# First MLP product of an encoder layer by one level of Strassen's scheme, with its result kept in DRAM between the two MLP products

## The reference

```python
h2 = rms_norm(x, norm_mlp_g)
x = x + jnp.square(jax.nn.relu(h2 @ w_mlp1)) @ w_mlp2
```

## Time and profile before

| | |
|---|---|
| runs | 2709.89, 2710.58, 2710.71 us; median 2710.58 us |
| profiled execution | 2709.54 us, of it a span of 2708.0 us that the records cover |
| PE busy | 2679.5 us (99%), weight loads 2322.8 us (86%) |
| DVE busy | 1210.4 us (45%) |
| ACT busy | 967.7 us (36%) |
| POOL busy | 150.9 us (6%) |
| granted TensorE clock | 0.999 |

### The profile page before, as it was taken

How to read it: one execution, slowest core, us unless ns; L and a number is a source line. 1 busy time by engine, 2 the same in 40 slices (tenths; PEclk the granted TensorE clock), 3 DMA queues, 4 the chain that set the end, 5 groups by cost and what they waited for, 6 DMA issues and landing times.

```text
span 2708.0 us, 39414 instructions
## 1 busy us (share of the span) xinstructions
PE 2679.5 (99%) x14690; PEld 2322.8 (86%) x14690; DVE 1210.4 (45%) x2015; ACT 967.7 (36%) x1645; POOL 150.9 (6%) x246
## 2 busy tenths in 40 slices
PE   7999999999999999999999999999999999999998
PEld 6888888889888888888888888888888888888887
DVE  4335433364333643345353534544445444544733
ACT  5554245443454434543352425211221122111531
POOL 3001000100001000100100010000000000000000
PEclk9999999999999999999999999999999999999999
DMA  3122122221222221221433222111111111111122
GB/s 112 25 32 71 42 71 32 31 73 43 62 32 33 71 74 31 33 54 59 183 120 119 87 86 62 40 39 39 38 33 39 38 39 39 39 39 39 33 67 64
DMA packets 174756, 153.10 MB, mean 57 GB/s; under 512 B 12352, under 2 KB 153216, under 8 KB 174624
## 3 DMA queue, kind: packets, MB, share of 16 engines
q1 hardware_dynamic: 156672, 95.05, 12.8%
q0 software_dynamic: 15872, 56.20, 7.4%
q10 hardware_dynamic: 2080, 0.14, 0.1%
HBM read 127.44 MB, written 23.74 MB: 56 GB/s over the span
## 4 chain that ended last, share of the span: by engine, by line
PE 97%; DVE 1%; ACT 1%; issue 1%; DMA 0%; SPq 0%; POOL 0%; ACTq 0%; DVEq 0%; POOLq 0%
PE bank L771 28%; PE bank L773 28%; PE bank L772 28%; PE bank L886 2%; PE bank L867 1%; PE bank L969 1%; PE bank L956 1%; PE bank L877 1%; PE bank L929 1%; PE bank L965 1%; PE bank L854 1%; PE bank L841 1%; PE bank L839 1%; DVE act_lo L1907 0%; PE bank L794 0%
## 5 line engine op out<-in xcount | busy, mean ns | idle before, releaser
L771 PE MATMUL bank<-act_hi,w_hi 128*128 128x512 f32 (+1 forms) x3192 | 1175.1, 368 | 0.7 <-DVE act_lo L1586 0.7
L773 PE MATMUL bank<-act_hi,w_lo 128*128 128x512 f32 (+1 forms) x3192 | 1131.9, 355 | 0.0
L772 PE MATMUL bank<-act_lo,w_hi 128*128 128x512 f32 (+1 forms) x3192 | 1131.2, 354 | 0.0
L773 PEld LDWEIGHTS bank<-act_hi,w_lo 128*128 128x128 f32 x3192 | 602.4, 189 | 86.4
L771 PEld LDWEIGHTS bank<-act_hi,w_hi 128*128 128x128 f32 x3192 | 603.7, 189 | 77.9 <-DVE act_lo L1586 0.9
L772 PEld LDWEIGHTS bank<-act_lo,w_hi 128*128 128x128 f32 x3192 | 604.6, 189 | 73.7
L1144 ACT ACTIVATE w_hi<-w_raw 128x1024 fp32r<-128x1024 f32 (+1 forms) x173 | 178.9, 1034 | 407.4 <-PE bank L773 387.1
L1561 DVE TENSOR_TENSOR w_lo<-w_raw,w_hi 128x1024 fp32r<-128x1024 f32 (+1 forms) x175 | 209.9, 1200 | 179.3 <-ACT w_hi L1144 178.4
L1960 DVE TENSOR_TENSOR work<-bank,work 128x512 f32<-128x512 f32 (+1 forms) x384 | 226.6, 601 | 129.4 <-PE bank L773 126.4
L771 PE MATMUL bank<-u_hi,w_hi 128*128 128x512 f32 (+1 forms) x768 | 272.3, 355 | 0.0
L772 PE MATMUL bank<-u_lo,w_hi 128*128 128x512 f32 (+1 forms) x768 | 272.0, 354 | 0.0
(11 more groups left out here) (262 smaller groups left out, 2476.6 us busy)
## 6 DMA issues: line engine op xcount, KB each, us to landing
w_raw<-in_w_in_dram SPq DMA_DIRECT2D x76, 512.0 KB
w_raw<-in_w_mlp_dram SPq DMA_DIRECT2D x64, 512.0 KB
work<-gate_scratch POOLq DMA_DIRECT2D x16, 640.0 KB, 5.6
gate_scratch<-work POOLq DMA_DIRECT2D x15, 640.0 KB, 3.3
work<-weight_scratch POOLq DMA_DIRECT2D x12, 640.0 KB, 5.9
oa_scratch<-work POOLq DMA_DIRECT2D x8, 640.0 KB, 4.7
work<-oa_scratch POOLq DMA_DIRECT2D x8, 640.0 KB, 12.6
x_in<-in_x_sample_dram SPq DMA_DIRECT2D x8, 512.0 KB, 7.7
```

Of the source, the lines that this page charges most:

```text
L771: nc.tensor.matmul(out, wh, rh, start=first and k == 0, stop=False, skip_group_check=True)
L772: nc.tensor.matmul(out, wh, rl, start=False, stop=False, skip_group_check=True)
L773: mm = nc.tensor.matmul(out, wl, rh, start=False, stop=k == kt - 1, skip_group_check=True)
```

## The change

With the 1024 inputs, the hidden features and the tokens each cut in two halves, a product of 2 x 2 blocks takes seven products of sums of blocks instead of eight. Here one pair i of hidden tiles (2 x 128 features), all 1280 tokens and all 1024 inputs is such a 2 x 2 product. There are 16 pairs and so 112 products g; each has 4 input tiles, 128 features and 640 tokens as 2 x 320 columns: 4 x 2 x 3 = 24 matmuls of 320 columns.

The seven products (numbered m as Strassen's) need sums and differences of the halves of h (x times `g_mlp`) and of the weights:

- Activations, once: `x_rows` lists the two halves; DVE (`piece_sum`) makes them for m = 4, 3 and 1, POOL for m = 7 and 6 (eight additions of 128 x 640), m = 2 and 5 are halves of h as they are. ACT makes the high parts (`piece_high`) and DVE the low parts (`piece_low`). They lie where `act_hi` and `act_lo` were; for m = 4 and 2 in rows 8 to 15 of `work`, and most of these are made during the eight tiles of `merged @ w_out`.
- Weights, for each product: two raw slabs of a pair lie in `w_raw` and `raw_1` (which is slot 0 of `w_hi`). `weight_sum` (DVE, 128 x 512), `weight_high` (ACT) and `weight_low` (DVE) fill one of three slots of `ring`, two products ahead. SP loads the next pair's slabs, `w_raw` first, once the last weight sum of the pair is made.
- Results: four quarters of a pair lie in `kept`, four rows of 640 in `work` rows 16 and 17. A product is in two PSUM banks; with 8 banks four products can be in flight. ACT copies the first use (`kept_copy`), DVE adds or subtracts the others (`added`). A finished quarter gets max and `r_bc` from DVE (`finals`), is squared by ACT, and POOL stores it to `u_scratch` in DRAM.
- x + merged @ w_out is stored to `x1_scratch` during the eight tiles and h is written over it; x is loaded back to `xres` in 14 half rows, seven at g = 56 and seven at g = 108. In `mlp_round` DVE waits for all of them.
- The second product follows in 16 rounds of two slabs. Each round's 256 rows of u (1280 KB) are loaded from DRAM by POOL, split by ACT (`u_highs`) and DVE (`u_lows`). Round 0's are loaded at g = 106; round 1's and 2's behind the last product and the last stores.
- The sum of squares is now in `r_bc`, and its matmuls (`squares_summed`) use banks 6, 7 and 6; PE waits for ACT's Ln before each reuse.

The core of the diff:

```diff
+            for i in range(PAIRS):
+                for m in (1, 0):
+                    if i:
+                        sp.wait_ge(sw_sum, sums_of(7 * i - 1) + 1)
...
+                    sp.dma_start((w_raw if m else raw_1)[:].rearrange("p (k n) -> p k n", n=P),
+                                 w_1[:, :, (2 * i + m) * P:(2 * i + m + 1) * P]).then_inc(raw_loaded[m], 16)
...
+                def part(a, j):
+                    hi, lo = x_operand(m, a)
+                    out = bank[2 * (g % 4) + j][:, 0:320]
+                    wh, wl = w[:, 0, a * P:a * P + P], w[:, 1, a * P:a * P + P]
+                    nc.tensor.matmul(out, wh, hi[:, j, :], start=a == 0, stop=False, skip_group_check=True)
+                    nc.tensor.matmul(out, wh, lo[:, j, :], start=False, stop=False, skip_group_check=True)
+                    return nc.tensor.matmul(out, wl, hi[:, j, :], start=False, stop=a == 3, skip_group_check=True)
...
+            s_product(0)
+            pe.wait_ge(x1_acc, KT + 4)
+            squares_summed(0, 6)
+            squares_summed(1, 7)
+            s_product(1)
+            pe.wait_ge(w2_read, 2)
+            squares_summed(2, 6)
+            s_product(2)
+            pe.wait_ge(w2_read, 4)
+            for g in range(3, PRODUCTS):
+                s_product(g)
...
+            for g in range(PRODUCTS + 1):
+                if g:
+                    kept_copy(g - 1)
+                if g == 1:
+                    root_part(0, 6)
+                    root_part(1, 7)
...
+                if g + 2 < PRODUCTS:
+                    weight_high(g + 2)
+                if g < 4:
...
+                    for pair in range(4):
+                        piece_high((1, 7, 6, 5)[g], pair)
...
+            for g in range(PRODUCTS + 1):
+                if g + 2 < PRODUCTS:
+                    weight_sum(g + 2)
...
+                if g:
+                    added(g - 1)
+                    finals(g - 1)
+                if 0 < g and g + 2 < PRODUCTS:
+                    weight_low(g + 2)
...
+                if g == PRODUCTS - 1:
+                    dve.wait_ge(sp_done, PRODUCTS)
+                    split_low(N_D, 0)
+                    u_lows(0, 0)
+            dve.wait_ge(x1_back, 32 * (KT - 1))
...
+                        if e == 0 and c == 0 and not last:
+                            u_lows(i + 1, 1 - par)
...
+            load_u(1, 1)
+            load_u(2, 0)
```

More of the change, by code:

```diff
@@ L198, in encoder @@
         assert pos[0] <= MAP_BYTES, pos[0]
-        bank = [ctx.enter_context(nc.psum_tensor(f"bank{i}", [P, 512], F32)) for i in range(8)]
+        banks = ctx.enter_context(nc.psum_tensor("banks", [P, 8, 512], F32))
+        bank = [banks[:, i, :] for i in range(8)]
         def dram(name, shape):
@@ new lines, in raw_part, with sums_of, x_rows @@
+        def raw_part(m, half):
+            t = w_raw if m else raw_1
+            return t[:].rearrange("p (a h n) -> p h a n", h=2, n=P)[:, half, :, :]
+        def sums_of(g):
+            i, q, m = product(g)
+            return 5 * i + sum(len(weight_parts(product(7 * i + r)[2])) == 2 for r in range(q + 1))
+        def x_rows(m, a):
+            return {4: ((2 * a + 1, 0), (2 * a, 0)), 2: ((2 * a, 0),), 3: ((2 * a, 1), (2 * a + 1, 1)),
+                    1: ((2 * a, 0), (2 * a + 1, 1)), 7: ((2 * a + 1, 0), (2 * a + 1, 1)),
+                    6: ((2 * a, 0), (2 * a, 1)), 5: ((2 * a + 1, 1),)}[m]
@@ new lines, in _ @@
+            left = 0
+            for g in range(PRODUCTS):
+                i, q, m = product(g)
+                for row, slab, side in leaving(g):
+                    left += 1
+                    pool.wait_ge(s_square, left + 1)
+                    pool.sem_inc(pool_passed, 1)
+                    r0 = (2 * i + slab) * P
+                    pool.dma_start(u_d[r0:r0 + P, 640 * side:640 * side + 640], kept[row]).then_inc(row_stored[row], 16)
+                if g == 7 * 8:
+                    for k in range(KT - 1):
+                        back(k, 1 - k % 2)
+                if g == PRODUCTS - 6:
+                    for r in range(4):
+                        pool.wait_ge(row_stored[r], 16 * 9)
+                    pool.wait_ge(sp_done, PRODUCTS - 4)
+                    pool.sem_inc(pool_passed, 1)
+                    pool.dma_start(u_raw0, u_d[0:2 * P, :].rearrange("(e p) t -> p e t", p=P)).then_inc(u_loaded[0], 16)
+                if g == PRODUCTS - 4:
+                    pool.wait_ge(sp_done, PRODUCTS - 2)
+                    pool.sem_inc(pool_passed, 1)
+                    for k in range(KT - 1):
+                        back(k, k % 2)
@@ new lines, in kept_copy @@
+            def kept_copy(g):
+                i, q, m = product(g)
+                if q > 2:
+                    return
+                row = KEPT[i][("s4", "s2", "s3")[q]]
+                act.wait_ge(sp_done, g + 2)
+                if g == 0:
+                    act.wait_ge(x1_acc, KT + 4)
+                if i:
+                    act.wait_ge(row_stored[row], 16 * i + 16)
+                A(kept[row].rearrange("p (j n) -> p j n", j=2), banks[:, 2 * (g % 4):2 * (g % 4) + 2, 0:320], ACT.Copy
+                  ).then_inc(s_copied, 1)
@@ new lines, in finals, with u_lows @@
+            def finals(g):
+                i, q, m = product(g)
+                for row, slab, side in leaving(g):
+                    dve.wait_ge(n_r, 2)
+                    dve.wait_ge(s_evac, 6 * i + q + 1)
+                    v_.scalar_tensor_tensor(out=kept[row], in0=kept[row], scalar=0.0, in1=r_bc[:, 640 * side:640 * side + 640],
+                                            op0=ALU.max, op1=ALU.mult).then_inc(s_final, 1)
+            def u_lows(i, par):
+                hi, lo = u_part(par)
+                for e in range(2):
+                    dve.wait_ge(u_high, 2 * i + e + 2)
+                    v_.tensor_tensor(lo[:, e, :], u_source(i, par)[:, e, :], hi[:, e, :].bitcast(F32), ALU.subtract).then_inc(u_low, 1)
```

569 lines of the change are left out of this document (422 added, 147 removed).

## The result

The changed kernel takes **2695.86 us** (median of 5 runs, 2694.42 to 2696.91) against 2710.58 (5 runs, 2709.56 to 2710.83): ratio 0.9947, 95% interval 0.9935 to 0.9958, 14.7 us faster. The forecast was 2692, its range 2677 to 2712.

What follows compares the result with a forecast made beforehand. PE's own work was taken to bound the kernel. The MLP: 393.8 + 440.5 + 2.5 + 2 + 19 + 8.7 + 1.5 = 868 us against 886.4, giving a time of 2692 us, range 2677 to 2712.

Steps and rivals of the forecast that it cites:

- Part 1, the matmuls: First product: 2688 matmuls of 320 columns at 0.1465 us, 393.8 us instead of 440.5, saving 46.7 us.
- the line through 256 and 512 columns: PE's matmul steps in the earlier trace: 0.42 ns a column plus a fixed 12 to 13 ns; 320 columns take 0.1465 us.
- The rival with the weight loads as the pace: First product: weight loads at 0.158 us each set the matmul pace, 31 us more, time 2723; chance 3%.
- Part 2, the pairs: Steady pairs, 24.6 us of PE each: DVE (18.2) and ACT (9.6) stay hidden, slabs land in time; nothing charged.
- Its price for a late slab: Raw weight loads in the pairs: each microsecond of landing over 8.1 costs 15 us; that rival had 13%.
- Part 3, the start: Opening of the first product: PE waits for pieces from DVE and ACT, 19 us in all, 14.7 without slow POOL.
- POOL's price: Opening: a 640-column POOL addition takes 1.6 us alone, a fifth of that pace beside DVE; m = 7's last sum at 21.3.
- the losses of 1.7 and 0.4: Opening: PE loses 1.7 us at product 0 for DVE's piece 3 of m = 4, and 0.4 before product 4.
- The lists without the slow neighbour: Opening: PE's losses from the engines' instruction lists if POOL is not slowed beside DVE, 14.7 us.
- the neighbour: Opening: POOL slowed beside DVE work with two SBUF inputs, the difference between 19 and 14.7 us; 4.3 us.
- Part 4, between the products: From first to second product: PE loses 2.7 us before round 0 and 6 us in it for u of round 1; 8.7.

Runs made afterwards that it cites:

- the filled wait: Changed kernel with 60 matmuls of 320 columns, result unread, put into PE's 9.7 us wait before the third sum of squares: 2695.83 us.
- the two mends: Changed kernel with POOL's eight additions moved to DVE and u of round 1 loaded with u of round 0: 2683.87 us, ratio 0.9902.
- the last kernel: Against the two mends: u of round 0 split before w2's slab, and DVE's chunk 0 additions before the second slab's low part: 2683.74 us.

## Why the prediction was right, point by point

- **Part 1, the matmuls: right.** 23 steps from 1663.36 to 1666.73 are 0.1465 us each, as read off the line through 256 and 512 columns. The matmuls of the first product cost 393.8 us. The rival with the weight loads as the pace is out: the steps are 0.1465 and not 0.158, though PEld is busy for 360.00 of 360 us in the pairs.
- **Part 2, the pairs: right.** The prediction let a slab land within 8.1 us, the two runs with late slabs give 8.3. The room was 4.1 us and not 2 because ACT began 4.2 us behind the issue, where the row of another stage had 6.1. Its price for a late slab, 15 us for each microsecond, was near: 2.1 us a pair made 37 us, 17 each. PE's waits are 29.8 us of that; each costs another 0.25 us before the steps are at full pace again (3.5 us in all), and three of the 14 waits are followed by some ten matmuls each at the half clock (3.7 us in all).
- **Part 3, the start: 19 us forecast, 15.1 measured, and the mechanism was the wrong way round.** Both halves of the sum were wrong, and that they cancel in good part is luck. The step that failed is POOL's price, "If POOL gets a fifth of its pace beside such DVE work": POOL's additions took 2.08 us each, against the 1.6 that the prediction had for POOL alone, so that m = 7's last sum was ready at 10.3 us (1673.65) and not at 21.3; it was DVE that lost, from 0.82 to 2.1 for each addition. From one row, in which POOL lost and DVE kept its 1.23, I made a rule for work with another ratio of lengths. The loss therefore came at the first Ln (9.7, forecast 4.1) and not at the last (1.2, forecast 5.7). The low parts in DVE's list made the waits that were forecast, only shorter (1.2 and 3.0, forecast 3.4 and 3.8), and the losses of 1.7 and 0.4 did not come. By the run without POOL's additions the two halves can be told apart. The lists without the slow neighbour were forecast at 14.7 us and cost 5.7; the neighbour was forecast at 4.3 and cost 9.4 in waits, 8.4 in time. The one was 9 us too much, the other 5 too little.
- **Part 4, between the products: 8.7 forecast, 8.1 measured**, in part by luck. 2.4 before round 0 (forecast 2.7), behind `u_lows(0)` as it said. In the round 1.5 + 4.2 = 5.7 (forecast 6): the 4.2 stand behind `u_lows` that waited for u of round 1, as it said; the 1.5 stand behind a slab of w2 that ACT could start on only 7.0 us after its issue (2079.01 to 2086.00), which the forecast did not have.
- **What the sum left out: the clock.** Behind the 9.7 and the 3.0 us wait, and in round 0, runs of matmuls are 0.267 us (320 columns), 0.213 (256) and 0.427 (512) apart instead of 0.1465, 0.1195 and 0.227: some 23 such steps in the opening and some 26 between the products, about 3 us over at each end. With them and 1.5 us not accounted for, against waits that were 4.5 us shorter than forecast, the MLP took 870.8 us and not 868. The runs' median was 3.9 us above the forecast; the other 1.1 lie outside the MLP. The first eight of these steps cost nothing, as the filled wait showed. The prediction also read the earlier trace rows as a wait inside the MLP, where PE had none; nothing in its sum hangs on that.

## What to carry to other kernels

When a new stage of PE is fed by pieces made just in time, add up the list of the engine that makes them over the whole opening; the waits that PE shows there are symptoms, and moving the one that is named moves the wait. Before giving additions to an idle engine, ask what they do to the neighbour that is already the bound: here eight additions less on DVE cost it more time than they saved, and taking them back brought 5.4 us. Where a value goes to DRAM and back, the first reads of the next stage want buffers of their own, asked for before the last stores are due, and where that place is crowded with transfers, as it is here, changes of order alone may bring nothing: two of them there brought nothing over the two mends.

## What the hardware did that was not expected

- DVE's instructions of two SBUF inputs over 640 columns (float32) took 2.1 us beside POOL's of the same kind and 0.82 alone; POOL's took 2.08. The Trainium skill, "GPSIMD Engine Reference", section Specifications, says that the SBUF interfaces are shared and that such DVE instructions contend. The trace agrees: DVE lost a factor of 2.6 here, and 2.9 in a low part of 512 columns (2.00 instead of 0.69). Both engines got through one addition in 2.1 us, as if they took turns, one for one; that is read off the equal steps and not tested, and so is what POOL itself lost, since no row has its addition of 640 columns alone.
- Behind some waits the granted clock fell to half: 0.267 us for 320 columns and 0.427 for 512 are one column a cycle at 1.2 GHz, to the last digit. The Trainium skill, "TensorE: Matmul & The Clock Gate", section Part 1, says that this clock gate stands at full or at half rate and never between; the steps agree. The length of the wait alone does not tell whether it happens. Behind the same wait of 2.4 us before round 0 the matmuls of 512 columns were 0.23 us apart in the changed kernel and 0.43 in the one with the slabs one product later. Of 14 waits of some 2.1 us in the one with the slabs two products later, three were followed by the half clock. Three waits of 1.71, 0.56 and 1.71 us, in the last kernel, left the clock of their stretch at 1.00.
- Behind the wait of 9.7 us the matmuls were slow from the first on. Behind that of 3.0 us eight ran at full pace, and the half clock came 1.3 us after PE had begun again (1704.44; the steps grow from 1705.71 on). So full pace in the first matmuls behind a wait does not say that the clock will stay.
